# Weight matrices laid out block by block, and the sample attention worked out row by row with queries broadcast by TensorE

## What is computed

```
u    = rmsnorm(x) * norm_g
proj = u @ w_in                      # 1024 x 8704: lx lg | sb scg sh sg | q qg | merge gates 3 x 1024
xc   = conv4(lx);  h = RG-LRU scan(xc);      z_a = (h * silu(lg)) @ lru_wo
cy   = conv3(scg * sh);                      z_b = (silu(sg) * sb * cy) @ sconv_wo
p    = softmax(q . mem_k / sqrt(128));       z_c = ((p @ mem_v) * silu(qg)) @ xa_wo     # 4 heads of 128, 256 memory tokens
y    = (sig(g_a) z_a + sig(g_b) z_b + sig(g_c) z_c) @ w_out
out  = rmsnorm(x + y) * final_norm_g
```

## Time and profile before

| | before |
|---|---|
| device time, median of 3 runs | 766.17 us (765.93 to 766.66) |
| the profiled execution, device time | 765.93 us |
| span of its slowest core, core 7 | 764.4 us |
| spans of the 8 cores | 758.2 to 764.4 us |
| PE, DVE, ACT, POOL busy | 719.3, 403.8, 345.0, 246.4 us |
| loads converted on the way (queue q0) | 97760 packets, 31.60 MB, 39.7% of the 16 transfer engines |

### The profile page before, as it was taken

The page is one execution under the profiler, slowest core; times in us unless marked ns, Lnnn a source line. Parts: engine busy times, 40 slices in busy tenths (PEclk is TensorE's granted clock), DMA queues, the critical chain, the costliest instruction groups (busy, mean ns, idle before and its releaser), DMA issues.

```text
span 764.4 us, 12999 instructions; the slowest of 8 cores (758.2 to 764.4 us)
## 1 busy us (share of the span) xinstructions
PE 719.3 (94%) x4771; PEld 456.5 (60%) x4771; DVE 403.8 (53%) x386; ACT 345.0 (45%) x408; POOL 246.4 (32%) x303
## 2 busy tenths in 40 slices
PE   2889999989999989989999999999999999999995
PEld 1556656556566646646666666666666666665442
DVE  3354343846749638736976789842223122223765
ACT  4247379686696587687663211121111211112332
POOL 5555201201202102102114256553555464423221
PEclk9999999999999999999999999999999999999998
DMA  9999944412512332403324588865294849036933
GB/s 198 173 193 164 134 87 43 43 15 28 52 19 28 32 34 28 41 8 39 39 22 83 55 170 175 181 94 56 26 147 53 123 48 86 6 121 213 301 142 141
DMA packets 108601, 69.48 MB, mean 91 GB/s; under 512 B 94003, under 2 KB 96197, under 8 KB 108523
## 3 DMA queue, kind: packets, MB, share of 16 engines
q0 software_dynamic: 97760, 31.60, 39.7%
q1 hardware_dynamic: 10779, 37.06, 14.3%
HBM read 90.53 MB, written 9.82 MB: 131 GB/s over the span
## 4 chain that ended last, share of the span: by engine, by line
PE 85%; DMA 6%; ACT 4%; issue 2%; DVE 2%; POOL 1%; SPq 0%; POOLq 0%; ACTq 0%; DVEq 0%
PE PP L645 73%; PE PP L1227 8%; DMA R<-xp 3%; DMA R<-w_in 3%; PE PP L994 2%; ACT R L848 1%; PE PP L986 1%; DVE R L835 1%; ACT R L989 1%; ACT R L699 0%; POOL R L693 0%; POOL R L703 0%; PE PP L771 0%; PE PP L1122 0%; ACT R L832 0%
## 5 line engine op out<-in xcount | busy, mean ns | idle before, releaser
L645 PE MATMUL PP<-R 128*128 128x344 bf16 x4104 | 615.3, 311 | 6.8 <-ACT R L848 4.0
L645 PEld LDWEIGHTS PP<-R 128*128 128x128 bf16 x4104 | 401.7, 98 | 215.4 <-issue 16.2
L1179 ACT ACTIVATE R<-PP 128x688 f32<-128x688 f32 x72 | 53.6, 744 | 210.0 <-PE PP L645 205.2
L134 POOL DMA_DIRECT2D R<-w_in x68 | 61.5, 904 | 262.5 <-PE PP L645 250.7
L1188 DVE SCALAR_TENSOR_TENSOR R<-R,PP 128x688 f32<-128x688 f32 x72 | 62.3, 869 | 137.9 <-PE PP L645 130.0
L1227 PE MATMUL PP<-R 128*128 128x512 bf16 (+1 forms) x272 | 59.0, 379 | 0.0
L1192 POOL TENSOR_TENSOR R<-R 128x688 f32<-128x688 f32 x24 | 41.2, 1721 | 39.8 <-DVE R L1188 38.0
L1197 POOL TENSOR_TENSOR R<-R 128x688 bf16<-128x688 f32 x24 | 40.0, 1689 | 18.6 <-DVE R L1188 17.2
L1227 PEld LDWEIGHTS PP<-R 128*128 128x128 bf16 (+1 forms) x272 | 26.4, 97 | 32.2 <-issue 0.4
L835 DVE SCALAR_TENSOR_TENSOR R<-R 128x2048 f32<-128x2048 f32 x18 | 42.3, 2349 | 5.4 <-ACT R L832 4.2
L1236 ACT ACTIVATE R<-R 128x1024 f32<-128x1024 f32 (+1 forms) x17 | 18.0, 1057 | 46.3 <-DVE R L1231 46.3
(11 more groups left out here) (133 smaller groups left out, 579.5 us busy)
## 6 DMA issues: line engine op xcount, KB each, us to landing
R<-w_in POOLq DMA_DIRECT2D x68, 256.0 KB, 5.1
R<-xp SPq DMA_DIRECT2D x32, 512.0 KB, 6.6
R<-ck SPq DMA_DIRECT2D x16, 512.0 KB, 4.7
y_p<-R SPq DMA_DIRECT2D x16, 512.0 KB, 3.0
R<-cv POOLq DMA_DIRECT2D x16, 256.0 KB, 7.5
R<-w_out POOLq DMA_DIRECT2D x8, 256.0 KB, 7.8
R<-xa_wo POOLq DMA_DIRECT2D x14, 128.0 KB, 4.1
R<-lru_wo POOLq DMA_DIRECT2D x8, 192.0 KB, 4.8
```

Of the source, the lines that this page charges most:

```text
L134: eng.dma_start(out=out, in_=in_).then_inc(sems[semkey], 16)
L645: return lambda e: e.matmul(ps.ap[:, b * 512:b * 512 + BLK], lhs(k), rhs[:, k, c:c + BLK], start=(k == 0), stop=(k == nk - 1))
L1179: G.act(lambda e, ps=pg[u], th_=th_: e.activation(out=b3(th_.ap), in_=pv(ps), func=AF.Tanh, scale=0.5), UW, [pg[u].tok], [th_.tok], Px - E ...
```

## The change

All weight blocks are laid out on the host so that a block is 128 rows, one for each partition: `w_in` becomes 68 blocks of 128 x 1024, `lru_wo` and `sconv_wo` 8 of 128 x 768, `xa_wo` 8 of 128 x 512, `xa_wk` and `xa_wv` one of 128 x 4096, and the two gate matrices of branch A are one tensor `lru_wab`. `w_out` stays. The planner's transfer rate goes from 240e3 to 280e3 and the factor 1.18 goes away.

The sample attention takes another form. `ck` and `cv` come in their natural layout, and a load takes two runs of 512 f32 for each partition (two halves of the memory tokens) in place of one of 1024. Queries are transposed head by head to 16 rows (`qs`, 16 x 512, four transposes in place of one). For every sample one matmul with 16 rows of contraction and 512 columns brings its query to all 128 partitions in a PSUM tile; DVE multiplies the keys with that. Two transposes of the score tile take the place of the small transfer. Values: for every sample 8 matmuls with a 128 x 128 piece of the values as weights and one column of probabilities, four samples into one PSUM tile; `Os`, its adds, its four transposes and the padding of `Pm` go away. There is room for six more value tiles in place of five.

```diff
-                a, n = max(dmafree[q], end + 0.8), t.dma[1] / 240e3
+                a, n = max(dmafree[q], end + 0.8), t.dma[1] / 280e3
...
-    w_in = din("w_in", [D, IN_COLS])
+    w_in = din("w_in", [IN_COLS // 128, 128, D])
...
         def wload(ap, prio):
-            k = ap.shape[1]
+            k = ap.shape[1] // 128
             hw = Handle(w2ring if 2 <= state["nw"] < 6 else wring)
-            G.dma("pool", [(lambda: hw.ap[:, 0:k * 128].rearrange("p (k c) -> p k c", k=k), ap)], k * 65536 * 1.18, [], [hw.tok], prio, None)
+            G.dma("pool", [(lambda: hw.ap[:, 0:k * 128], ap)], k * 65536, [], [hw.tok], prio, None)
...
         def w_in_cols(c0):
-            return w_in.rearrange("(k p) c -> p k c", p=128)[:, :, c0:c0 + 128]
+            return w_in[c0 // 128]
...
-                G.dma("pool", [(v, src.rearrange("(k p) c -> p k c", p=128))], 2097152, [], [m.t], P - 20, sem)
+                G.dma("pool", [(m.ap, src[:, :])], 2097152, [], [m.t], P - 20, sem)
...
-            if hd < 3:
-                return
             P += 8
-            tq = m_tq.ap.rearrange("p (c b h) -> p c b h", c=2, h=4)
-            for c in range(2):
-                G.dve(lambda e, c=c: e.tensor_copy(tq[:, c].rearrange("p b h -> p h b"), og[:, :, T:TT]), 64,
-                      [t_og[i][4] for i in range(4)], [m_tq.t], P)
             ps = Handle(PS)
-            G.pe([lambda e: e.transpose(ps.ap.bitcast(BF16)[:, 0:128], m_tq.ap, identb)], 0.1, [m_tq.t, m_identb.t], [ps.tok], P)
-            G.dve(lambda e: e.tensor_copy(qs, ps.ap.bitcast(BF16)[:, 0:128]), 128, [ps.tok], [m_qs.t], P)
+            G.pe([lambda e: e.transpose(ps.ap.bitcast(BF16)[0:TS, 0:128], og[:, hd, T:TT], identb)], 0.1,
+                 [t_og[hd][4], m_identb.t], [ps.tok], P)
+            G.dve(lambda e: e.tensor_copy(qs[0:TS, hd * 128:(hd + 1) * 128], ps.ap.bitcast(BF16)[0:TS, 0:128]), 128,
+                  [ps.tok], [m_qs.t], P)
...
         def sample_scores(P, dP):
             kring, prring = ring("Kb", m_Kb, True), ring("prod", [m_prod])
-            for s in range(TS):
-                k_, pr_ = Handle(kring), Handle(prring)
-                P1 = P + s * dP
-                G.dma("sp", [(lambda k_=k_: k_.ap, ck[s])], 524288, [], [k_.tok], P1 - EV, None)
-                G.dve(lambda e, k_=k_, pr_=pr_: e.tensor_tensor(
-                    out=pr_.ap.rearrange("p (m d) -> p m d", m=8), in0=k_.ap.rearrange("p (m d) -> p m d", m=8),
-                    in1=qs.unsqueeze(1).to_broadcast([128, 8, 128]), op=ALU.mult), 1024, [k_.tok, m_qs.t], [pr_.tok], P1)
+            for b in range(TS):
+                k_, pr_, ps = Handle(kring), Handle(prring), Handle(PS)
+                P1 = P + b * dP
+                G.dma("sp", [(lambda k_=k_: k_.ap.rearrange("p (c f) -> p c f", c=2), ck[b].rearrange("(c m) f -> m c f", c=2))], 524288,
+                      [], [k_.tok], P1 - EV, None)
+                G.pe([lambda e, b=b, ps=ps: e.matmul(ps.ap[:, 0:512], identb[0:TS, b:b + 1].to_broadcast([TS, 128]), qs[0:TS, :],
+                                                     start=True, stop=True)], 0.25, [m_identb.t, m_qs.t], [ps.tok], P1)
+                G.dve(lambda e, k_=k_, pr_=pr_, ps=ps: e.tensor_tensor(
+                    out=pr_.ap.rearrange("p (c f) -> p c f", c=2), in0=k_.ap.rearrange("p (c f) -> p c f", c=2),
+                    in1=ps.ap[:, 0:512].unsqueeze(1).to_broadcast([128, 2, 512]), op=ALU.mult), 1024,
+                    [k_.tok, ps.tok], [pr_.tok], P1)
...
-            G.dma("sp", [(Sall[0:64, 128:256], Sall[64:128, 0:128])], 32768, [m_Sall.t], [m_Sall.t], P2, "sall")
+            G.pe([lambda e, c=c: e.transpose(ps.ap[0:64, c * 128:(c + 1) * 128], m_Sall.ap[:, c * 64:(c + 1) * 64], ident)
+                  for c in range(2)], 0.4, [m_Sall.t, m_ident.t], [ps.tok], P2)
...
         def sample_values(P, dP):
-                def mm(c, g, r=r, vs=vs, ps=ps):
-                    return lambda e: e.matmul(ps.ap[32 * g:32 * g + 32, 0:512], Pm[:, c, r * 4 + g, :],
-                                              vs[g].ap[:, c * 512:(c + 1) * 512], start=(c == 0), stop=(c == 1))
-                G.pe([mm(c, g) for c in range(2) for g in range(4)], 0.6, [v.tok for v in vs] + [m_Pm.t], [ps.tok], P1)
+            for g in range(4):
+                ps = Handle(PS)
+                for bi in range(4):
+                    b = g * 4 + bi
+                    v_ = Handle(varing if b % 4 == 0 or b == 1 else vbring)
+                    P1 = P + b * dP
+                    G.dma("pool", [(lambda v_=v_: v_.ap.rearrange("p (c f) -> p c f", c=2), cv[b].rearrange("(c m) f -> m c f", c=2))],
+                          524288, [], [v_.tok], P1 - EV, None)
+
+                    def mm(hd, c, b=b, bi=bi, v_=v_, ps=ps):
+                        return lambda e: e.matmul(ps.ap[:, bi * 4 + hd:bi * 4 + hd + 1],
+                                                  v_.ap[:, c * 512 + hd * 128:c * 512 + (hd + 1) * 128],
+                                                  Pm[:, c, b * 4 + hd:b * 4 + hd + 1], start=(c == 0), stop=(c == 1))
+                    G.pe([mm(hd, c) for hd in range(4) for c in range(2)], 0.55, [v_.tok, m_Pm.t], [ps.tok], P1)
```

More of the change, by code:

```diff
@@ L561, in build_program @@
         m_a2 = side("a2", 0, TT, F32)
[L562 to L569, removed]
+        m_qs = Mem("qs", PERM, XW, BF16)
+        m_Sall = Mem("Sall", PERM + 1024, 128, F32)
+        m_Pm = Mem("Pm", PERM + 1536, 128, BF16)
+        m_Es = Mem("Es", PERM + 1792, 256, F32)
+        m_Ps = Mem("Ps", PERM + 2816, 256, F32)
+        m_thS = Mem("thS", PERM + 3840, NJS * TS, F32)
+        m_acS = Mem("acS", PERM + 3840 + NJS * TS * 4, NJS * TS, F32)
         S = Sched(nc)
@@ L1068, in build_program @@
         m_Va = [Mem(f"Va{i}", m_wo.off + 12288 + i * 2048, 1024, BF16) for i in range(2)]
-        m_Vb = [Mem(f"Vb{i}", m_wo.off + i * 2048, 1024, BF16) for i in range(5)]
-        m_Os = Mem("Os", m_wo.off + 10240, 512, F32)
+        m_Vb = [Mem(f"Vb{i}", m_wo.off + i * 2048, 1024, BF16) for i in range(6)]
         def sample_scores(P, dP):
             kring, prring = ring("Kb", m_Kb, True), ring("prod", [m_prod])
-            Sall, sm = m_Sall.ap, m_sm.ap
-            for s in range(TS):
-                k_, pr_ = Handle(kring), Handle(prring)
-                P1 = P + s * dP
-                G.dma("sp", [(lambda k_=k_: k_.ap, ck[s])], 524288, [], [k_.tok], P1 - EV, None)
-                G.dve(lambda e, k_=k_, pr_=pr_: e.tensor_tensor(
-                    out=pr_.ap.rearrange("p (m d) -> p m d", m=8), in0=k_.ap.rearrange("p (m d) -> p m d", m=8),
-                    in1=qs.unsqueeze(1).to_broadcast([128, 8, 128]), op=ALU.mult), 1024, [k_.tok, m_qs.t], [pr_.tok], P1)
-                G.dve(lambda e, s=s, pr_=pr_: e.tensor_reduce(out=Sall[:, s * 8:(s + 1) * 8], in_=pr_.ap.rearrange("p (m d) -> p m d", m=8),
+            Sall = m_Sall.ap.rearrange("p (c b h) -> p c b h", c=2, b=TS)
+            for b in range(TS):
[9 more added lines that the diff above has]
+                    [k_.tok, ps.tok], [pr_.tok], P1)
+                G.dve(lambda e, b=b, pr_=pr_: e.tensor_reduce(out=Sall[:, :, b, :], in_=pr_.ap.rearrange("p (c h d) -> p c h d", c=2, h=4),
@@ L1090, in sample_scores @@
+            sm = m_sm.ap
+            G.dve(lambda e: e.tensor_reduce(out=sm[0:64, 0:1], in_=ps.ap[0:64, 0:256], axis=AX.X, op=ALU.max), 256, [ps.tok], [m_sm.t], P2)
             G.dve(lambda e: e.tensor_scalar(out=sm[0:64, 0:1], in0=sm[0:64, 0:1], scalar1=-SCALE, scalar2=None, op0=ALU.mult), 1,
                   [m_sm.t], [m_sm.t], P2)
[L1092 to L1093 removed]
+            G.act(lambda e: e.activation(out=m_Es.ap[0:64, :], in_=ps.ap[0:64, 0:256], func=AF.Exp, scale=SCALE, bias=sm[0:64, 0:1],
+                                         accum_out=sm[0:64, 1:2]), 480, [ps.tok, m_sm.t], [m_Es.t, m_sm.t], P2, EXP, psum=True)
@@ L1101, in sample_scores @@
                   for c in range(2)], 0.4, [m_Ps.t, m_ident.t], [ps2.tok], P2)
-            for r in range(4):
-                G.dve(lambda e, r=r: e.tensor_copy(
-                    Pm[:, :, r * 4:r * 4 + 4, r * 4:r * 4 + 4],
-                    ps2.ap[:, 0:128].rearrange("p (c b h) -> p c b h", c=2, h=4)[:, :, r * 4:r * 4 + 4, :]), 32, [ps2.tok], [m_Pm.t], P2)
+            G.dve(lambda e: e.tensor_copy(m_Pm.ap, ps2.ap[:, 0:128]), 128, [ps2.tok], [m_Pm.t], P2)
         def sample_values(P, dP):
@@ L1109, in sample_values @@
             varing, vbring = ring("Va", m_Va, True), ring("Vb", m_Vb, True)
[L1110 to L1112 removed]
+            Pm = m_Pm.ap.rearrange("p (c q) -> p c q", c=2)
+            for g in range(4):
                 ps = Handle(PS)
[L1114 to L1129 removed]
@@ L1130, in sample_values @@
-            P1 = P + 16 * dP
-            ps = Handle(PS)
-            G.pe([lambda e, hd=hd: e.transpose(ps.ap[:, hd * 128:(hd + 1) * 128], Os[:, hd * 128:(hd + 1) * 128], ident)
-                  for hd in range(4)], 0.8, [m_Os.t, m_ident.t], [ps.tok], P1)
```

(12 more changed lines are left out.)

68 lines of the change are left out of this document (25 added, 43 removed).

## The result

The changed kernel takes 776.93 us (776.05 to 779.01), the kernel before, timed beside it, 766.41 us: a ratio of 1.0136 [1.0109, 1.0164], 10.5 us slower where 1.8 us faster was forecast.

A forecast was written before the change was run, and what follows sets the result against it. PE was taken as the bound behind the head, transfers as what holds it up in the head. -6.5 + 3.4 + 0.3 + 0.2 - 2.6 + 3.1 + 0.3 = -1.8 us gave 764.4 us, range 759 to 770.5.

The forecast's parts named there:

- The head, -6.5: Head: cheaper weight blocks free the transfers; PE starts 1.5 us earlier and regains 5.0 us of lost time.
- rival (a): Head: new plan, ACT's order or the tile-block chain sets PE's pace; 2.2 us slower, 768.4 us; chance 0.13.
- The start of PE: Head: PE begins 1.5 us earlier, bounds 0.5 and 2.5, through POOL's issues and the first block's transfer.
- The broadcasts, +3.4: Sample scores: 16 query broadcast matmuls of 512 columns at 0.215 us each on a full PE, 3.4 us.
- The values, +3.1 and -2.6: Sample values: 128 one-column matmuls at 0.024 us add 3.1 us; removed groups and transposes save 2.6 us.
- rival (b): Sample values: one-column matmuls bound by 97 ns weight loads, 12.4 us in place of 3.1; 773.7 us; chance 0.07.
- Transposes of the scores, +0.3: Sample scores: two transposes of the score tile on PE, 0.27 us like those of the probabilities.
- Queries, +0.2: Head: three more small query transposes on PE cost 0.2 us.
- PSUM and DVE, +0.3: Score stage: broadcasts hold a PSUM tile until DVE has multiplied; 0.3 us, bounds 0 and 4.
- rival (c): Score stage: the held PSUM tile stalls PE, 4 us in all, 768 us; chance 0.10.

The follow-up runs named there:

- w_cvsplit: The kernel before with the new weight block layout, and each value tile loaded as two runs per partition: 762.94 us, ratio 0.9926.
- a_c240: The changed kernel with the planner's two old constants (240e3 bytes per us, factor 1.18): 773.44 us, ratio 1.0059.
- w_only: The kernel before with the new weight block layout alone, old planner constants and sample attention: 767.26 us, ratio 0.9998.
- s_only: The kernel before with the new sample attention alone, old weight layout and planner constants: 777.4 us, ratio 1.014.

## Why the prediction was wrong

By the ratios, and with 766.4 us for the kernel before, the way from before to after goes in three steps that differ by one part each: to w_cvsplit -5.7 us (the layout, with the value tiles' loads), on to a_c240 +10.2 (the rest of the sample form), on to after +5.9 (the constants). Together 10.4; by the intervals each step is known to 2 or 3 us.

**The head, -6.5.** For the layout this term holds in size: -5.7, or -4.3 (w_cvsplit) to -5.6 (w_only) by the first w_out matmul. Its picture was too bright, so that the size is in part luck. A block costs 1.76 us in place of the 1.53 forecast, the tiles 1.67 us in place of 1.6 (46.0% x 66 us over 18.2 tiles of 0.52 MB), and the last full tile is squared at 58.9 us (60.2 in w_cvsplit), not near 50. The chain of block and tile keeps the step, as rival (a) said (20.5 us, in w_cvsplit 20.1, beside 21.2); the transfers are no longer full (0.88 in place of 1.01), and still each tile waits for a block. What the layout does give shows in PE's waits from 24.5 to 67.5 us: some 6 us before, 2.9 in w_cvsplit, 4.1 in the changed kernel (medians over the cores). What failed is the step from the layout to the whole change: I listed the new transfer estimates as part of rival (a), at 13 in 100, and put no price on them in the sum. They take the gain back (+5.9), in part through ACT's list, which (a) names, though the other way round: there squares were to stand behind copies, and what PE waits for are copies behind squares.

**The start of PE.** Forecast 1.5 us earlier. The first unit matmul of the changed kernel is at 26.05 us in the slowest core, beside 24.74; over the eight cores the medians are 24.3 and 24.5. The start gave next to nothing.

**The broadcasts, +3.4.** The term that was mis-sized. I took a pair of full-row score matmuls as the nearest row and wrote that nothing lies below 0.215 us; the surcharge lay above. Pieces of PE's timeline, counted from the start of each to the start of the next, put 5.9 us on the 16 broadcasts, of which 0.9 is the stall below, and the gaps ahead of them, 0.11 each, lengthen the unit matmuls' pieces. With 128 rows 2.9 us of it go; 16 x 0.215 would be 3.4, and where the other 0.5 stays I have not traced.

**The values, +3.1 and -2.6.** Right. The one-column matmuls, from PE's timeline:

```profile
567.22 0.34 PE L1113 MATMUL PP<-R 128*128 128x1 bf16 x8
567.42 2.49 PE L643 MATMUL PP<-R 128*128 128x344 bf16 x16
```

Eight of them hold PE for 0.20 us, 0.025 each, and all 128 for 3.26, by the same count of pieces. Each with a weight load listed at 96 ns: rival (b) is out. (So is, as the price of a stream of loads, the rule of the Trainium skill cited with it, TensorE: Matmul & The Clock Gate, section LDWEIGHTS: 0.025 us measured in place of 0.107.)

**Transposes of the scores, +0.3.** 0.22 measured. **Queries, +0.2.** 1 to 2 us are lost ahead of the merge: the last score matmul is 1.2 us later in a_c240 than in w_cvsplit and 1.8 in s_only than before, each by one execution. The query transposes are the new work there; the waits named at s_only are what grew, and no run tells the two apart.

**PSUM and DVE, +0.3.** PE's waits from 380 to 710 us, where the kernel before has none:

```profile
PE PP L1096 <- DVE R L1093: 1.0, 1, 1.0
PE PP L643 <- DVE R L1169: 0.9, 1, 0.9
PE PP L643 <- ACT R L846: 0.4, 2, 0.3
PE PP L643 <- DVE R L879: 0.3, 1, 0.3
```

The held tile shows once, at 0.9 us, so rival (c) was a quarter of its price. The 1.0 us of L1096 is a transpose of the probabilities that waits for the softmax on DVE; before, it had no wait (L1100), and I had put none in the sum.

The merge as a whole: unit matmuls' pieces 1.9 us longer (the gaps ahead of the broadcasts and the wait at L1096, less the gaps ahead of the removed matmuls), broadcasts 5.9, values 3.3, score transposes 0.2, and 2.6 removed, 8.7 us beside 8.6 measured; the forecast for these was 4.5. The rest of the miss is 5.9 for the constants, 0.8 for the layout and 1.4 for what the sample form loses ahead of the merge (10.2 - 8.6, less the 0.2 of the forecast), whose cause stays open: 4.1 + 5.9 + 0.8 + 1.4 = 12.2, the distance from -1.8 to +10.4.

## What to carry to other kernels

Where a planner or a scheduler reads estimates, a change of the estimates is an edit of its own, to be costed by itself: here a layout worth 0.74% came with two constants that took as much back. In this kernel a short-row matmul in a stream of full-row ones cost twice a full-row one, 0.43 us in place of 0.22, so it is to be priced with its weight load bare, and padded with zeros to full rows where that is free. And a time that stays the same is not a change that does nothing: read where the work ended and where the program ended, each for itself.

## What the runs showed of the hardware

POOL's closing drain is not constant. It took 3.11, 3.60, 3.93, 4.25 or 9.64 us, the same within 0.01 us on all eight cores of a kernel, and went with what POOL's queue had been given to load; with fewer and longer packets it was longer. What sets it stays open. It costs nothing at 4.25 us or less here, since the last stores are waited for beside it, and 4.5 us at 9.64.

A 512-column matmul with 16 rows and its weight load, among loads of 128 rows, cost 0.43 us of PE in place of 0.22, though the load's own listed duration is the same (0.09 and 0.10 us).
